# High and low input in one 512-column matmul for the gate/up and q/k products of a two-block model kernel

## The reference, cut to what matters

```python
def swiglu_ffn(x, w_gate, w_up, w_down):          # D_FF = 2816
    return (jax.nn.silu(x @ w_gate) * (x @ w_up)) @ w_down

x = x + 0.5 * swiglu_ffn(rmsnorm(x, ffn1_norm[l]), ...)
x = x + hybrid_mixer(rmsnorm(x, mix_norm[l]), ...)
x = x + 0.5 * swiglu_ffn(rmsnorm(x, ffn2_norm[l]), ...)
x = rmsnorm(x, final_norm[l])
...
q, k, v, f_logit, gate = _split(x @ w_in, [H * dh, H * dh, H * dh, H, D])   # FOX, H = 8, dh = 128
```

## Time and profile before

| | us |
|---|---|
| median of 3 runs | 749.05 (747.11 to 749.78) |
| the profiled execution | 747.19 |
| its span in the profile | 745.4 |
| TensorE busy | 722.1 |
| VectorE busy | 447.5 |
| ScalarE busy | 351.7 |
| HBM traffic | 126.77 MB read, 171 GB/s over the span |

### The profile page before, as it was taken

One profiled execution on the slowest core, in us unless ns is written; L12 is line 12 of the kernel. 1 busy time (PEld: TensorE's weight loads), 2 busy tenths in 40 slices (PEclk: granted clock), 3 DMA queues, 4 the chain that ended last, 5 costly groups with the idle time before them and its releaser, 6 DMA issues.

```text
span 745.4 us, 11354 instructions
## 1 busy us (share of the span) xinstructions
PE 722.1 (97%) x4596; PEld 650.0 (87%) x4596; DVE 447.5 (60%) x707; ACT 351.7 (47%) x457; POOL 73.0 (10%) x43
## 2 busy tenths in 40 slices
PE   7999999999999999999999999999999999987985
PEld 6999999988887889999999888889998988766874
DVE  5875656655476446656566655485543657893655
ACT  5643334535377546534434444466335444564351
POOL 4000000000001320000000000000017260420002
PEclk8999999999999999999999999999999999999997
DMA  8986455545355344645545574265545133631001
GB/s 246 351 351 262 169 176 190 198 170 197 142 189 207 113 174 153 240 173 187 203 169 172 180 270 173 110 229 195 197 170 193 58 113 113 226 113 56 1 1 57
DMA packets 20535, 128.37 MB, mean 172 GB/s; under 512 B 2416, under 2 KB 3312, under 8 KB 6160
## 3 DMA queue, kind: packets, MB, share of 16 engines
q1 hardware_dynamic: 20448, 127.70, 48.0%
q0 software_dynamic: 48, 0.13, 0.1%
HBM read 126.77 MB, written 1.05 MB: 171 GB/s over the span
## 4 chain that ended last, share of the span: by engine, by line
PE 93%; DVE 2%; ACT 2%; DMA 1%; POOL 1%; issue 1%; SPq 0%; DVEq 0%; POOLq 0%; ACTq 0%
PE ps L368 29%; PE ps L370 28%; PE ps L369 28%; PE ps L565 1%; DMA work<-in_xt 1%; PE ps L379 1%; PE ps L622 1%; PE ps L621 1%; PE ps L903 1%; PE ps L620 1%; DVE wlo L1364 1%; PE ps L736 1%; ACT whi L978 1%; PE ps L892 0%; PE ps L611 0%
## 5 line engine op out<-in xcount | busy, mean ns | idle before, releaser
L368 PE MATMUL ps<-xth,whi 128*128 128x256 f32 x832 | 237.3, 285 | 4.4 <-DVE wlo L1501 4.4
L369 PE MATMUL ps<-xtl,whi 128*128 128x256 f32 x832 | 236.6, 284 | 0.0
L370 PE MATMUL ps<-xth,wlo 128*128 128x256 f32 x832 | 236.6, 284 | 0.0
L978 ACT ACTIVATE whi<-raw 128x2048 fp32r<-128x2048 f32 x78 | 148.6, 1909 | 100.3 <-PE ps L370 97.6
L1364 DVE TENSOR_TENSOR wlo<-raw,whi 128x2048 fp32r<-128x2048 f32 x68 | 156.7, 2314 | 64.3 <-ACT whi L978 64.2
L368 PEld LDWEIGHTS ps<-xth,whi 128*128 128x128 f32 x832 | 161.0, 194 | 5.2 <-DVE xtl L1377 5.1
L369 PEld LDWEIGHTS ps<-xtl,whi 128*128 128x128 f32 x832 | 161.0, 194 | 0.1
L370 PEld LDWEIGHTS ps<-xth,wlo 128*128 128x128 f32 x832 | 160.9, 193 | 0.0
L368 PE MATMUL ps<-whi,xth 128*128 128x512 f32 (+1 forms) x304 | 122.8, 404 | 3.2 <-DVE xtl L1493 2.0
L370 PE MATMUL ps<-whi,xtl 128*128 128x512 f32 (+1 forms) x304 | 117.9, 388 | 0.0
L369 PE MATMUL ps<-wlo,xth 128*128 128x512 f32 (+1 forms) x304 | 117.5, 387 | 0.0
(11 more groups left out here) (209 smaller groups left out, 681.0 us busy)
## 6 DMA issues: line engine op xcount, KB each, us to landing
raw<-in_gu SPq DMA_DIRECT2D x41, 1024.0 KB, 4.8
raw<-in_dn SPq DMA_DIRECT2D x22, 1024.0 KB, 4.7
raw<-in_win SPq DMA_DIRECT2D x8, 1024.0 KB, 4.8
raw<-in_fqk SPq DMA_DIRECT2D x8, 1024.0 KB, 5.0
raw<-in_wout SPq DMA_DIRECT2D x4, 1024.0 KB, 4.9
raw<-in_fg SPq DMA_DIRECT2D x4, 1024.0 KB, 5.0
raw<-in_fv SPq DMA_DIRECT2D x4, 1024.0 KB, 4.7
raw<-in_fo SPq DMA_DIRECT2D x4, 1024.0 KB, 4.7
```

Of the source, the lines that this page charges most:

```text
L368: pe.matmul(o, xh, wh, start=start, stop=False)
L369: pe.matmul(o, xh, wl, start=False, stop=False)
L370: return pe.matmul(o, xl, wh, start=False, stop=stop)
L978: act.activation(whi[:, c % RING, 0:n], raw[:, c % RING, 0:n], ACT.Copy).then_inc(hi_ready, 1)
```

## The change

- The high and low inputs become one tensor `xt` with, for each k slice, the 256 high and then the 256 low columns; `xth` and `xtl` are views of it.
- A gate/up or q/k product of one k slice is now two matmuls (`both_halves`): high weights times high and low input side by side (512 columns, a whole bank), and low weights times the high input (256 columns) added to the second half. At the last k slice the order of the two is turned. A chunk is 32 matmuls. The other products keep `three`.
- The first half of the bank then holds high x high, the second half the sum of the two small parts, so gate and up need a bank each: chunk i of four takes banks 2i and 2i+1, all eight in turn. The rows of 1/rms move to bank 7 (`ROW`), the down products wait for `gu_read` of 20 chunks, chunk 3 waits for the row.
- Evacuation: ScalarE copies the second halves of both banks to SBUF (`cross`, 128 x 512) ahead of its `hi`; VectorE adds the first halves to them (128 x 512), and scales both in one operation with the row broadcast. `sg_sb` and `up_sb` become `gu_sb`.
- q/k: the same, with two pairs of banks (4/5 and 6/7) in place of four banks; ScalarE's copy and VectorE's sum (`qk_sum`) and its two scalings stand ahead of `hi` and `lo` of the next chunk. The forget gate's matmul moves from bank 4 to 6, the second block's row from bank 5 to 7.

```diff
+            def both_halves(bank, wh, wl, k, first, last):
+                x = xt[:, k, :, :].rearrange("p a s -> p (a s)")
+                small = ps[:, bank, S:2 * S], wl, xth[:, k, :]
+                if last:
+                    pe.matmul(*small, start=False, stop=False)
+                    return pe.matmul(ps[:, bank, :], wh, x, start=False, stop=True)
+                pe.matmul(ps[:, bank, :], wh, x, start=first, stop=False)
+                return pe.matmul(*small, start=False, stop=False)
...
-                    elif f == 1 and i == 3:
-                        pe.wait_ge(gu_read, NG + 1)
+                    elif i == 3:
+                        pe.wait_ge(row_ready, f + 1)
...
-                        m = three(ps[:, banks[u], u * S:(u + 1) * S], wh[:, w], wl[:, w], xth[:, k, :], xtl[:, k, :], k == 0, k == KD - 1)
+                        m = both_halves(2 * i + u, wh[:, w], wl[:, w], k, k == 0, k == KD - 1)
...
+                pe.wait_ge(gu_read, NG * f + 20)
                 for g in range(ND):
                     pe.wait_ge(ht_lo, ND * f + g + 1)
...
-                if h == 0:
+                if h == 1:
                     pe.wait_ge(f_order, 1)
-                if h == 1:
                     pe.wait_ge(row_ready, 3)
-                if h >= 4:
-                    pe.wait_ge(qk2_ready, 2 * (h - 3))
+                if h >= 2:
+                    pe.wait_ge(qk2_ready, 3 * (h - 2) + 1)
...
+                def cross(j, i):
+                    act.wait_ge(chunk_used, C_GU[f] + i + 1 + 4 * j)
+                    if not (isinstance(j, int) and f + j == 0 and i < 2):
+                        act.wait_ge(h_done, NG * f + i - 1 + 4 * j)
+                    act.activation(gu_sb[:, i % 2, :, :], ps[:, 2 * i:2 * i + 2, S:2 * S], ACT.Copy).then_inc(cross_copied, 1)
...
                     for i in range(4):
                         c = C_GU[f] + RING + i
+                        cross(j, i)
                         act.wait_ge(raw_landed[c % RING], 16 * (c // RING + 1) + 16 * j)
...
-                    dve.tensor_tensor(sg_sb[:, i % 2, :], ps[:, GU + i, 0:S], ffn_row, ALU.mult).then_inc(gate_scaled, 1)
...
-                    dve.tensor_tensor(up_sb[:, i % 2, :], ps[:, up_bank, S:2 * S], ffn_row, ALU.mult).then_inc(gu_read, 1)
+                    dve.wait_ge(cross_copied, NG * f + i + 1 + 4 * j)
+                    g = gu_sb[:, i % 2, :, :]
+                    dve.tensor_tensor(g, ps[:, 2 * i:2 * i + 2, 0:S], g, ALU.add).then_inc(gu_read, 1)
+                    dve.wait_ge(gu_read, NG * f + i + 1 + 4 * j)
+                    dve.tensor_tensor(g, g, ffn_row.unsqueeze(1).broadcast_to([P, 2, S]), ALU.mult).then_inc(gate_scaled, 1)
...
+                act.wait_ge(chunk_used, C_FQK + h + 1)
+                if h >= 2:
+                    act.wait_ge(qk2_ready, 3 * (h - 1))
+                bank = 4 + 2 * (h % 2)
+                act.activation(qk_sum[:, h % 2, :, :], ps[:, bank:bank + 2, S:2 * S], ACT.Copy).then_inc(cross_copied, 1)
                 hi(C_FQK + h + RING)
...
+                dve.wait_ge(chunk_used, C_FQK + h + 1)
+                bank = 4 + 2 * (h % 2)
+                dve.wait_ge(cross_copied, 2 * NG + h + 1)
+                dve.tensor_tensor(qk_sum[:, h % 2, :, :], ps[:, bank:bank + 2, 0:S], qk_sum[:, h % 2, :, :], ALU.add).then_inc(qk2_ready, 1)
+                dve.wait_ge(qk2_ready, 3 * h + 1)
+                dve.scalar_tensor_tensor(out=q2t[:, h, :], in0=qk_sum[:, h % 2, 0, :], scalar=SCALE2, in1=rstd_row, op0=ALU.mult, op1=ALU.mult).then_inc(qk2_ready, 1)
+                dve.tensor_tensor(k2t[:, h, :], qk_sum[:, h % 2, 1, :], rstd_row, ALU.mult).then_inc(qk2_ready, 1)
                 if C_FQK + h + RING < C_FO:
                     lo(C_FQK + h + RING)
```

More of the change, by code:

```diff
@@ L255, in build @@
         y_psum_t, y_hi, y_lo = sem("y_psum_t"), sem("y_hi"), sem("y_lo")
-        f_psum, f_order, f_neg, f_exp, f_ln, f_log, cum_ready, cum_hi, cum_lo = (
-            sem(n) for n in ("f_psum", "f_order", "f_neg", "f_exp", "f_ln", "f_log", "cum_ready", "cum_hi", "cum_lo"))
+        f_psum, f_order, f_neg, f_soft, f_log, cum_ready, cum_hi, cum_lo = (
+            sem(n) for n in ("f_psum", "f_order", "f_neg", "f_soft", "f_log", "cum_ready", "cum_hi", "cum_lo"))
         hot_ready, diag_ready, row_psum, row_ready = sem("hot_ready"), sem("diag_ready"), sem("row_psum"), sem("row_ready")
@@ L476, in gate_and_up @@
                     wh, wl = whi[:, c % RING, :], wlo[:, c % RING, :]
-                    if f == 1 and static and j == 0 and i == 0:
-                        steps, banks = [(k, u) for half in range(2) for u in range(2) for k in range(half * HALF, (half + 1) * HALF)], [b, GU + 3]
+                    if opening:
+                        steps = [(k, u) for half in range(2) for u in range(2) for k in range(half * HALF, (half + 1) * HALF)]
                     elif in_halves:
-                        steps, banks = [(k, u) for k in range(KD) for u in range(2)], [b, DOWN + 1 + i]
+                        steps = [(k, u) for k in range(KD) for u in range(2)]
                     else:
-                        steps, banks = [(k, u) for u in range(2) for k in range(KD)], [b, b]
+                        steps = [(k, u) for u in range(2) for k in range(KD)]
                     for k, u in steps:
-                        if f == 1 and static and j == 0 and i == 0:
+                        if opening:
                             if u == 0:
@@ L1026, in ffn @@
                 else:
+                    cross(0, 0)
                     hi(C_GU[f] + RING)
+                    cross(0, 1)
                     hi(C_GU[f] + 1 + RING)
-                    row(f, DOWN, ffn_row)
+                    row(f, ROW, ffn_row)
                 silu(0, 0)
@@ L1032, in ffn @@
                 for i in range(2, 4):
+                    cross(0, i)
                     hi(C_GU[f] + i + RING)
@@ L1044, in ffn @@
                 for i in range(2):
+                    cross(5, i)
                     hi(C_GU[f] + 20 + i + RING)
@@ L1604, in _ @@
             dve.wait_ge(f_psum, 1)
[L1605 removed]
+            dve.tensor_tensor(fz, ps[0:F2, 6, 0:S], rstd_row[0:F2, :], ALU.mult).then_inc(f_order, 1)
             dve.wait_ge(f_order, 1)
```

67 lines of the change are left out of this document (30 added, 37 removed).

## The result

The changed kernel takes 740.80 us, the median of 4 runs (739.55 to 742.84), against 748.08 for the kernel before (4 runs, 745.56 to 749.78). The ratio is 0.9914, 95% interval 0.989 to 0.9938: 6.4 us faster by the ratio, 7.3 by the medians, where 10.9 were forecast.

What follows compares the result with a forecast made beforehand. TensorE bounds the kernel, by number of matmuls times pitch. Profiled 747.19 us less 10.9 (815 products x 13.3 ns), all else hidden, gives 736.3; 1.9 more for the median gives 738.2, range 733 to 744.5.

Steps and rivals of the forecast that it cites:

- TensorE's pace is the time: In the changed stages, time is the number of matmuls times their pitch; other engines count only if later than TensorE.
- A matmul costs its columns and 13.3 ns at any width: On TensorE, columns at 2.4 GHz plus 13.3 ns: 120.0 ns at 256 columns, 226.7 at 512.
- the saving of a product: Gate/up and q/k: 360 ns falls to 346.7, so 13.3 ns for each of 815 products, 10.9 us.
- rival A: Each switch of width costs: 350 to 355 ns a product, gain 8.2 to 4.1 us, 740.9 to 744.9; chance 0.14.
- my own case: Steady 346.7 ns a product, everything else hidden: 738.2 us for the median, chance 0.69.
- The first two chunks: 32 gate/up products at the start: 8 wait for inputs and some 9 run at half clock, so these save nothing.
- Evacuation: FFN chunks: ScalarE +0.60 us, VectorE +0.54 to 4.09, both below 5.55 us of matmuls, so costed at nothing.
- Rival D: VectorE becomes the bound of the FFN stages if its turn, copy included, passes 5.76 us: 804 us, chance 0.03.
- Moved banks, q/k: Chunk 3's row wait has 2.5 us to spare in the first FFN; raised waits and q/k evacuation cost nothing.
- Rivals B and C: B: 256-column matmul behind 512 cheaper, 342 ns, 734.1, chance 0.12. C: product stays at 360 ns, 749, chance 0.02.
- The gap formula of the Trainium skill: Gap between warm matmuls of N/2.4 + 2.5 ns: gain 2.5 ns a product, 2 us in all, landing at 747.

## Why the prediction was right, and where it was off

**TensorE's pace is the time: right.** No new wait came, and the kernel with everything but the wide matmul is as fast as the one before, within 0.2%.

**A matmul costs its columns and 13.3 ns at any width: right while the width stays** (226.7 at 512, 173.4 at 384, 146.8 at 320; but 206.7, not 200.0, at 448), and wrong for what the change does, which is to alternate. The term that was mis-sized is the saving of a product: "I take the steady 346.7, between them", so 13.3 ns; it measured 360 - 352.5 = 7.5 in the steady stages. The traces bear out rival A, 350 to 355, to which I had given 0.14. That the time lies well within the range is owed to the range, which took in nearly all of A, and in part to the time before, 748.08 in these runs where the sum began at 749.05; my own case alone had 738.2. Some 31 products (chunk 2 and the warm part of the first two) had the full 13.3, the other 784 had 7.5: 0.4 + 5.9 = 6.3 us, against 6.4 measured by the ratio. The rows that spoke for it were there, 235 ns for the first matmuls behind a switch; I took them for an effect that dies, and where each matmul of 512 stands behind a switch it can't die. My reason, that the wide matmul leaves more room for the next weight load, is refuted: with 384 columns in the second matmul the excess grew to 13 ns.

**The first two chunks: right in kind.** The stretch at half clock gave nothing, and chunk 2 starts at 25.20 us where it was 25.10. In the other kernels it starts between 24.3 and 26.3, so a tenth is within what executions differ there.

**Evacuation: right**, to the hundredth for the three durations. Rival D had the wrong threshold, as the kernel with more evacuation shows: the bound is VectorE's 4.1 us of own work and not the turn with the copy in it, and behind it stand 11.8 us of reserve.

**Moved banks, q/k: right.** The row of the second FFN was copied by 300.62 us and chunk 3 started at 303.75, 3.4 and 2.3 us ahead of my reckoning, which had left out the 2.4 us gained by the end of the first FFN's gate/up chunks, with 3.1 us to spare. In q/k no wait for the sum shows either.

**Rivals B and C** did not occur. The gap formula of the Trainium skill (N/2.4 + 2.5 ns; TensorE: Matmul & The Clock Gate, Back-to-back issue gap), which the page gives for the isolated gap of a matmul, doesn't hold for these streams, in which each matmul has its own weight load: they show 13.3 ns over the columns at even widths of 256, 320, 384 and 512, and 22 behind a wide and 10.5 behind a narrow one when they alternate.

**What the traces show of the two speeds.** A stretch of wide and narrow in turn goes on in the pattern in which it begins, and the pattern changes only where something else comes: two matmuls of one width in a row, or other matmuls between. Chunk 2, with the same order of widths, slices and banks, ran at 346.6 to 347.1 in six kernels and at 352.9 to 354.2 in three (one of these three adds to the other half of the bank); in each of the nine the first pair had already been running in a pattern of that speed when it ended. With no such place in a stage, one speed holds through all its chunks; with one pair of narrow and one of wide neighbours in a chunk, the two speeds take turns. More evacuation, the shared slice, the half of the bank and the bank itself don't decide it.

**What stays open:** by what rule such a place picks the next pattern, and what in the hardware makes the patterns; and why 448 columns carry an excess without any change of width. No kernel took away the turned slices alone (the two that have none also add to the other half of the bank). Whether a stage of one program keeps its speed from one execution to the next was not tried, since each kernel has one trace.

## What to carry to other kernels

Fewer and wider matmuls on the same columns save the fixed part of each one left out, here 13.3 ns, but don't count on it in full where neighbours differ in width, and measure the pitch at the width that you want (448 columns fell out of line). Group equal widths (here sixteen and sixteen), which cost nothing but the order of issue. Look at the pitch chunk by chunk: a mean of 350 over a stage was 347 and 353 in turn. And before pricing an engine that gets more work as a new bound, compare its own instructions with the period, and then ask how many chunks of reserve the ring holds.

## What was not expected of the hardware

Starts of matmuls alternating between 512 and 256 columns fall into repeating patterns: 230/117 ns over one product, 231/113/232/118 over two (both 346.7), and 236/113/233/117/241/120 over three (353.3). With nothing between but such pairs a stretch kept its pattern for 110 us, over all chunks; in the kernel with k outside the speed changed at the end of every chunk (5.56 and 5.64 us in turn).
